# The output product of a convolution branch as seven block products, with its weights' parts kept in DRAM

## The reference, cut to what matters

```
h = rmsnorm(x);  proj = h @ W_in + b_in            # conv_val | conv_gate | pool_in | gate_a | gate_b
u  = causal_dwconv_31(conv_val * sigmoid(conv_gate))
ya = silu(layernorm(u)) @ conv_w_out               # branch A: the product that is changed
yb = (pooling branch) * scale
merged = sigmoid(gate_a) * ya + sigmoid(gate_b) * yb
x = x + merged @ mix_w_out;  x = x + gdfn(rmsnorm(x));  out = rmsnorm(x)
```

## Time and profile before

| | us |
|---|---|
| median of three runs | 1289.86 |
| their range | 1289.23 to 1290.2 |
| the profiled execution | 1289.33 |
| its span in the trace | 1287.3 |

### The profile page before, as it was taken

How to read it: one execution, slowest core, us unless ns; L and a number is a source line. 1 busy time by engine, 2 the same in 40 slices (tenths; PEclk the granted TensorE clock), 3 DMA queues, 4 the chain that set the end, 5 groups by cost and what they waited for, 6 DMA issues and landing times.

```text
span 1287.3 us, 15571 instructions
## 1 busy us (share of the span) xinstructions
PE 1270.3 (99%) x5766; PEld 1053.8 (82%) x5766; DVE 1022.8 (79%) x1163; ACT 479.5 (37%) x691; POOL 871.1 (68%) x579
## 2 busy tenths in 40 slices
PE   8999999999999999999999999999999999999997
PEld 8888888888888778877888888888888888888887
DVE  5898989999999784589677767677666779887975
ACT  6211221213234580143445343343344445424551
POOL 4536637665787833478739977877887876567861
PEclk9999999999999999999999999999999999999999
DMA  9411121214334372344212322332232259868923
GB/s 352 149 33 49 34 82 49 82 33 164 99 99 149 130 290 69 114 155 164 102 39 90 123 107 92 121 121 88 93 117 107 90 175 361 332 243 290 367 87 131
DMA packets 66408, 179.26 MB, mean 139 GB/s; under 512 B 4896, under 2 KB 13088, under 8 KB 62496
## 3 DMA queue, kind: packets, MB, share of 16 engines
q1 hardware_dynamic: 61888, 167.82, 36.2%
q10 hardware_dynamic: 4448, 10.49, 2.2%
HBM read 137.14 MB, written 41.16 MB: 139 GB/s over the span
## 4 chain that ended last, share of the span: by engine, by line
PE 90%; DVE 4%; ACT 2%; issue 2%; POOL 1%; DMA 1%; SPq 0%; DVEq 0%; POOLq 0%; ACTq 0%
PE ps L2494 30%; PE ps L2495 30%; PE ps L2496 30%; DMA cv<-in_x 1%; DVE h_lo L2092 1%; POOL w_lo L1037 1%; PE ps L2558 1%; ACT cv L1244 0%; PE ps L2548 0%; DVE cv L2083 0%; ACT cv_r L1626 0%; DVE hi_f L2004 0%; POOL w_lo L1170 0%; DVE res L2271 0%; DVE res L2187 0%
## 5 line engine op out<-in xcount | busy, mean ns | idle before, releaser
L2494 PE MATMUL ps<-h_lo,w_hi 128*128 128x512 f32 (+1 forms) x900 | 348.0, 387 | 4.5 <-DVE h_lo L1838 1.9
L2496 PE MATMUL ps<-h_hi,w_hi 128*128 128x512 f32 (+1 forms) x900 | 345.9, 384 | 0.0
L2495 PE MATMUL ps<-h_hi,w_lo 128*128 128x512 f32 (+1 forms) x900 | 345.9, 384 | 0.0
L2494 PEld LDWEIGHTS ps<-h_lo,w_hi 128*128 128x128 f32 x900 | 169.0, 188 | 41.8 <-DVE h_lo L1838 3.1
L2496 PEld LDWEIGHTS ps<-h_hi,w_hi 128*128 128x128 f32 x900 | 169.0, 188 | 33.9
L2495 PEld LDWEIGHTS ps<-h_hi,w_lo 128*128 128x128 f32 x900 | 169.1, 188 | 33.1
L1918 DVE SCALAR_TENSOR_TENSOR ps<-tmp,par,ps 128x512 f32<-128x512 f32 x224 | 158.5, 750 | 0.0
L965 POOL TENSOR_SCALAR w_hi<-raw 128x1024 fp32r<-128x1024 f32 x32 | 36.5, 1141 | 156.1 <-issue 127.5
L2494 PE MATMUL ps<-ga_r,w_hi 128*128 128x512 f32 (+1 forms) x303 | 117.4, 388 | 0.3 <-POOL w_lo L1170 0.3
L2496 PE MATMUL ps<-cv_r,w_hi 128*128 128x512 f32 (+1 forms) x303 | 117.1, 386 | 0.0
L2495 PE MATMUL ps<-cv_r,w_lo 128*128 128x512 f32 (+1 forms) x303 | 117.0, 386 | 0.0
(11 more groups left out here) (308 smaller groups left out, 2721.3 us busy)
## 6 DMA issues: line engine op xcount, KB each, us to landing
raw<-in_wstream SPq DMA_DIRECT2D x54, 512.0 KB, 3.5
tmp<-in_wffn SPq DMA_DIRECT2D x14, 1024.0 KB, 4.7
g_kept<-res SPq DMA_DIRECT2D x21, 512.0 KB, 2.8
res<-in_wffn SPq DMA_DIRECT2D x10, 1024.0 KB, 4.8
ga_r<-g_kept SPq DMA_DIRECT2D x18, 512.0 KB, 7.0
h_lo<-g_kept SPq DMA_DIRECT2D x17, 512.0 KB, 7.5
res<-in_xT SPq DMA_DIRECT2D x7, 1024.0 KB, 5.8
g_kept<-raw SPq DMA_DIRECT2D x12, 512.0 KB, 2.9
```

The costliest lines, as they stand in the source:

```text
L2494: nc.tensor.matmul(out, a_hi, b_lo, start=start, stop=False, skip_group_check=onto)
L2495: nc.tensor.matmul(out, a_lo, b_hi, start=False, stop=False, skip_group_check=onto)
L2496: return nc.tensor.matmul(out, a_hi, b_hi, start=False, stop=stop, skip_group_check=onto)
```

## The change

Branch A's output product becomes seven block products too, for four pairs of output tiles: 28 of 12 matmuls. What it needs:

- **Weights.** The sums S and the parts of all 28 are made during the first stages: eight half blocks (`PREP_SLOTS`), each loaded by SP, four sums and seven low parts on GpSimd (`prep_sum_of`, `prep_low`) on 128 by 256 values, stored by SP into `prep_kept_t`. The places between the splits are fixed by `PREP_SLOTS` and `PREP_ENDS`. During the product SP loads each block product's high and low parts (2 x 256 KB) into a ring of four.
- **High parts of the chunks** of the first stages go from GpSimd to ScalarE (`split_high`), and so do part of the prep's (`prep_highs`).
- **Order on TensorE.** P1 for the four pairs, P2 for the four, then P6, P5, P7, P4, P3 for pairs 0 and 1, and the same for 2 and 3. In SP's order `gates_back(0)` waits until all twelve low parts of z are made.
- **Data.** The T operands of z are made by VectorE, their high parts by ScalarE. VectorE forms the four result quarters from the banks (`conv_u2_of`, `conv_c22`, `conv_c21`, `conv_c12`) and merges half tiles; the gates (`a_kept_t`) come back from DRAM in 256 KB pieces.
- The mixer's block products get other places, and their sums for the first two blocks are made earlier.

```diff
+PREP_SLOTS, PREP_ENDS = (5, 7, 9, 11, 14, 18, 21, 24), (6, 7, 10, 11, 15, 19, 23, 25)
+PREP_BY_ACT = (1, 2, 4, 6, 7)
+PREP_SEQ = (P1, P2, P4, P5, P7, P6, P3)
+PREP_FIRST, PREP_LAST = PREP_SEQ[:3], PREP_SEQ[3:]
...
+            def keep_prep(x, *ps):
+                i, h = x // 2, x % 2
+                for p in ps:
+                    k = prep_n(x, p)
+                    sp.wait_ge(prep_lo, k + 1)
+                    sp.dma_start(prep_dram[CONV_SEQ.index((p, i)), :, :, h * (HALF // 2):(h + 1) * (HALF // 2)],
+                                 prep_place(k).bitcast(f32).rearrange("p (t n) -> p t n", t=2)).then_inc(prep_kept[k % PREP_PLACES], 16)
...
-            load_chunks(2, FIRST_GATE // 2 - 1)
+            load_prep(0)
+            load_early(N_FIRST, FIRST_GATE - 2)
             sp.wait_ge(w_split, FIRST_GATE - 3)
             load_weights(FIRST_GATE - 2)
+            keep_slot(FIRST_GATE - 4)
             sp.wait_ge(gb_done, PAIR0)
             sp.wait_ge(y_kept, 16 * 2)
             sp.dma_start(y_dram[:, 0:2, :], tiles(res, 0, 2)).then_inc(y_kept, 16)
...
+            def load_conv(*ops):
+                for p, i in ops:
+                    n = conv_op(p, i)
+                    r = n - GATE_OPS
+                    sp.wait_ge(f_used, n - MIX_SLOTS + 1)
+                    for t, w_t in enumerate((w_hi, w_lo)):
+                        sp.dma_start(conv_ring(w_t, n).bitcast(f32), prep_dram[r, :, t, :]).then_inc(cv_w[r % MIX_SLOTS], 16)
...
+            load_conv((P6, 0), (P6, 1))
+            for j in range(4):
+                gates_back(j)
+            load_conv((P5, 0), (P5, 1), (P7, 0))
...
+            def prep_first(x):
+                pool.wait_ge(prep_raw, 16 * (x + 1))
+                prep_sum_of("S1", x)
+                prep_low(x, P1)
+                prep_sum_of("S3", x)
+                prep_low(x, P2)
+                prep_sum_of("S2", x)
+                prep_low(x, P4)
+                prep_sum_of("S4", x)
...
-            pairs(N_OUT, (((f_post, gate_posted(GP - 2, "c12")),),
-                          ((s1_out, gates_read(GP - 1, 1)), (f_post, gate_posted(GP - 1, "c21")))), co_m, h_hi, h_lo,
-                  lambda h, k: (z_lo, KT * h + k + 1))
+            for i in range(MP):
+                pe.wait_ge(*((f_post, gate_posted(GP - 2, "c21")), (f_post, gate_posted(GP - 2, "c12")),
+                             (s1_out, gates_read(GP - 2, 1)), (s1_out, gates_read(GP - 1, 1)))[i])
+                conv_product(P1, i, ready=(lambda k: (z_lo, k + 1)) if i == 0 else None)
+            for i in range(MP):
+                pe.wait_ge(f_v1, GP + i + 1)
+                conv_product(P2, i, False, ready=(lambda k: (z_lo, 4 + k + 1)) if i == 0 else None)
```

More of the change, by code:

```diff
@@ new lines, with prep_n, prep_stores, conv_posted @@
+PREP_TOPS = NP7 * len(PREP_SLOTS) - PREP_HIGHS
+def prep_n(x, p):
+    return NP7 * x + PREP_SEQ.index(p)
+def prep_stores(place, n=NP7 * len(PREP_SLOTS)):
+    return sum(k % PREP_PLACES == place for k in range(n))
+CONV_POSTS = [(what, a + i) for a in (0, 2) for group in (("u2",), ("u3", "c22"), ("c21",), ("c12",))
+              for i in range(2) for what in group]
+def conv_posted(what, i):
+    return len(POSTS) * GP + CONV_POSTS.index((what, i)) + 1
+MERGES = [(what, a + i) for a in (0, 2) for what in ("c11", "c22", "c21", "c12") for i in range(2)]
@@ L424, in gate_out @@
         def gate_out(c, h):
-            if c == KT - 1:
-                return tile(ga, c, *span(h))
-            return odd_out[:, :] if h and c % 2 else second_half(hi_f, h)
+            return odd_out[:, :] if h and c % 2 and c < KT - 1 else second_half(hi_f, h)
         def pooled(c):
@@ new lines, in _ @@
+            conv_u2_of(0)
+            conv_t_low("T3")
+            conv_u2_of(1)
+            conv_t_low("T4")
+            merge("c11", 0)
+            merge("c11", 1)
+            for i in range(2):
+                conv_c22(i)
+                merge("c22", i)
+            for i in range(2):
+                conv_c21(i)
+                merge("c21", i)
+            for i in range(2):
+                conv_c12(i)
+                merge("c12", i)
+            conv_u2_of(2)
+            merged_low(0, 0)
@@ new lines, in _ @@
+            merged_low(1, 0)
+            conv_u2_of(3)
+            merge("c11", 2)
+            merge("c11", 3)
+            merged_low(2, 0)
+            merged_low(3, 0)
+            merged_low(4, 0)
+            merged_low(6, 0)
+            for k in range(4):
+                mix_t_sum_of("T1", k)
+            conv_c22(2)
+            merge("c22", 2)
+            conv_c22(3)
+            merge("c22", 3)
+            conv_c21(2)
+            merge("c21", 2)
+            conv_c21(3)
+            merge("c21", 3)
@@ L2739, in _, with conv_product @@
-            pairs(N_OUT, (((f_post, gate_posted(GP - 2, "c12")),),
-                          ((s1_out, gates_read(GP - 1, 1)), (f_post, gate_posted(GP - 1, "c21")))), co_m, h_hi, h_lo,
-                  lambda h, k: (z_lo, KT * h + k + 1))
+            def conv_product(p, i, first=True, ready=None):
+                n = conv_op(p, i)
+                r = n - GATE_OPS
+                pe.wait_ge(cv_w[r % MIX_SLOTS], 32 * (r // MIX_SLOTS + 1))
+                hi, lo = conv_ring(w_hi, n), conv_ring(w_lo, n)
+                for k in range(4):
+                    if ready:
+                        pe.wait_ge(*ready(k))
+                    mm = three(conv_bank(p, i), hi[:, k * P:(k + 1) * P], lo[:, k * P:(k + 1) * P],
+                               *conv_moving(PRODUCTS[p].partition("*")[2], k), first and k == 0, k == 3, not first)
+                mm.then_inc(f_used, 1)
```

799 lines of the change are left out of this document (551 added, 248 removed), and 4 rows, old and new, of the table MIX_ADDS.

## The result

The changed kernel takes 1307.81 us in the median (1304.77 to 1308.96, 4 runs), the kernel before 1289.78 (1289.23 to 1290.2, 4 runs). The ratio is 1.0138, 95% interval 1.0126 to 1.015: it is slower by 18 us, where 7 us less was forecast, and outside the range. One execution of all those reported here, of the kernel of experiment 7, took 2132.56 us at a mean granted clock of 0.556, and no comparison uses it.

A forecast was written before the change was run, and what follows sets the result against it. TensorE, 99% busy, was taken to bound the kernel. From 1289.3 us the terms -10.9, -1.0, -0.8, +5.0, +0.7 and +0.5 gave 1282.8, left at 1283; 8-in-10 range 1277 to 1289, the forecast's own 1280 to 1286.

The forecast's parts named there:

- the sum's silent start: Whole kernel: the sum starts from the profiled 1289.3 us and takes off 48 matmuls at 0.227 us each.
- sign of being wrong as a whole: TensorE's waits from 30 to 650 us summing to more than 10 us or to less than 3.
- Term 1: Branch A's output product: 336 matmuls instead of 384, at 0.227 us each, -10.9 us.
- Term 2: Start of branch A's output product: the 1.04 us wait on a low part of z goes, -1.0 us.
- Term 3: Entry to the mixer's products: the 0.87 us wait for low parts of weights shrinks through earlier sums, -0.8 us.
- Term 4: T loads on SP: prep stores delay them, VectorE runs late, TensorE stalls at `gate_u2(0)` and the mean matmul, +5.0 us.
- Term 5: Supply of the new product: P5's weights land late behind SP's wait at `gates_back(0)`, +0.7 us, bounds 0 and 4.
- Term 6: First stages: GpSimd's added prep work fits its idle time, splits almost all in time, +0.5 us, bounds 0 and 3.
- The slower rival: New product: DMA starves the block products, deciding from about 270 GB/s down; 18 us more at 250, end 1300; chance 0.10.
- The first rival: T loads: they are no loss, term 4 is 0 to 2 us, time 1276 to 1280; chance 0.22.
- a fit of the Trainium skill: T loads: 2.0 us plus bytes over 436 GB/s, store 4.4 us, both loads 6.8, term 4 about 1.5, end 1279.3.

The follow-up runs named there:

- experiment 7: Kernel of experiment 6 plus one 256 KB copy within DRAM for each block product of the new product: 1286.82 us, ratio 0.9981 to the kernel before.
- aligned kernel: Changed kernel with its SBUF tensors allocated in another order, so every product operand starts at a multiple of 128 bytes: 1288.08 us, ratio 0.9993 to the kernel before.
- experiment 5: Aligned kernel with SP's loads of the T operands ahead of the three prep stores: 1283.05 us, ratio 0.9949 to the kernel before.
- experiment 6: Kernel of experiment 5 with P5's weights for pairs 0 and 1 issued ahead of the first four gate loads: 1281.77 us, ratio 0.993 to the kernel before.
- experiment 10: Kernel of experiment 6 with half block 3's three first high parts on ScalarE and pooled tile 6 reloaded later: 1295.25 us, ratio 1.0045 to the kernel before.
- experiment 11: Kernel of experiment 6 with half block 3's last four parts made behind chunk 13's split, not chunk 11's: 1285.11 us, ratio 0.9968 to the kernel before.
- the first kernel: First of two kernels of matmuls alone, 22 groups of 24 at different byte offsets: 0.228 us per matmul with both operands at 32, 0.233 with weights elsewhere.

## Why the prediction was wrong

For each stage, what TensorE's starts lie apart beyond 0.227 us, added up over its timeline (only steps over 0.26 us: waits, the restarts behind them, and the slow clock), in us:

| stage (us) | before | changed | aligned | + T loads early | + P5 early |
|---|---|---|---|---|---|
| first stages, 30 to 345 | 0.1 | 0.8 | 2.5 | 2.6 | 2.8 |
| 345 to 370 | 0 | 1.9 | 5.05 | 0 | 0 |
| rest of the gates, to 467 | 3.7 | 3.5 | 3.6 | 3.6 | 3.6 |
| new product, to 545 | 1.7 | 3.4 | 3.0 | 3.5 | 2.3 |
| mixer, to 640 | 2.45 | 2.5 | 1.75 | 1.8 | 1.7 |
| later, to 1250 | 1.7 | 0.2 | 1.8 | 1.5 | 1.5 |

- **The step that failed** is the sum's silent start: "1289.3" less 48 matmuls takes for granted that the other 5718 keep their 0.227 us. They don't. Changed and aligned kernel differ by 21.3 us of span; the aligned one loses 5.4 us more to waits (17.7 against 12.3 in the table), so the longer distance costs 26.7 us, 4.7 ns for each matmul. The starts say the same: between 30 and 1250 us the mean of all steps under 0.26 us is 0.2320 us in the changed kernel and 0.2269 in the aligned one. The prediction named the cost of each edit of work and left out one that moves no work: 8 columns more on two tensors. Its own sign of being wrong as a whole, waits over 10 us or under 3 between 30 and 650 us, could not catch this: they are 8.4 us.
- **Term 1** holds with the addresses right: 48 matmuls less, 0.227 us each.
- **Term 2** (-1.0): the wait is gone; the new product's first matmuls start without one.
- **Term 3** (-0.8): 2.45 to 1.75, -0.7.
- **Term 4** (+5.0): +5.05 in the aligned kernel, at the named place and from the named cause, as experiment 5 shows. That the size fits so well is in part luck. The loads went out at 301.98 us, as forecast; but the store had taken 4.6 us (6.4 forecast), and VectorE could start only 11.4 us behind the loads' issue (8.1 forecast). VectorE's first T sum began 9.0 us later than before the change and `gate_u2(0)` ended 6.7 us later (5 forecast), so 2.3 us were given back (2.5 forecast). TensorE itself came 2.7 us later than before, so with the 0.7 us of slack its wait is 3.4 us, and 1.65 of slow clock behind it, which the prediction didn't have, fill up the sum. At the mean matmul nothing more was lost.
- **Term 5** (+0.7): mis-sized. The stage lost 3.0 us where before, with its one wait, lost 1.7: +1.3, and with term 2's 1.0 taken out +2.3; the P5 wait that was named is 0.8 to 1.3 us of it, and the rest are waits of 0.1 to 0.3 on weights, with the slower steps behind them.
- **Term 6** (+0.5): mis-sized, +2.4, and from three causes. "The others have over 1 us" counted GpSimd's operations but not when the half blocks land: half block 3 landed 4.4 us after its issue in the kernel of experiment 6, 2.6 of them idle on GpSimd, and the splits behind it cost 0.7 us at 155 and 166 us. At 251 us 0.8 us go to a small product whose read-out stands on ScalarE behind the high parts that the change put there. And at 336 us 0.9 us go to a low part of a split that took 4.4 us where 2.4 were counted.
- **Together**, with the measured terms: 1289.3 - 10.9 - 1.0 - 0.7 + 5.05 + 2.3 + 2.4 = 1286.5; the profiled execution of the aligned kernel has 1287.38. So had the addresses been kept, the median, 1288.08 us, would have been in the range for 8 in 10 (1277 to 1289), but 5 us above the forecast, outside the forecast's own 1280 to 1286, and no gain that can be told from none.
- **The rivals.** The slower rival gave chance 0.10 to an outcome that came, but by the wrong mechanism: DMA averages 305 GB/s over the stage in the changed kernel (475 to 550 us) and 326 in that of experiment 6, above the 270 that it needed to decide, though single stretches lie under it (263 GB/s from 467 to 475 us in experiment 6). VectorE held TensorE up in the new product once, 0.8 us at 549.7 us of the changed kernel. The first rival, no loss at the T loads, is out by experiment 5. The prediction set beside it a fit of the Trainium skill (DMA: Bandwidth & Descriptors, Anatomy of one DMA) that the page gives for DMAs issued by GpSimd; here SP issues them. The 4.4 us that it gives for the store are near the 4.6 measured, the 6.8 for the two loads are not near 11.4.

## What to carry to other kernels

When a diff changes the size of any SBUF tensor, compare the start addresses of each product's moving operand and weights before and after, keep their difference at a multiple of 256 bytes, and read the distance of matmul starts before looking for waits: the busy share hardly tells (99% before, 98% after). A wait put into one engine's queue stops all that stands behind it, so a copy or a store moved there is priced by what it waits for, and late operands cost twice when TensorE's pause brings the slow clock.

## What the runs showed of the hardware

Two things were not expected. **The distance between fast float32 matmuls of 512 columns depends on how the moving operand and the weights lie to each other in a partition:** 0.227 us (0.229 with a group's first matmuls) where the starts differ by a multiple of 256 bytes, or 16 bytes less, and 0.231 to 0.237 in nearly all other groups, up to 4%, with nothing else running. The exceptions leave the full rule open: 0.229 at a difference of 64 (modulo 256) in three groups, with 0.233 in two others, and 0.229 at one of 124 in the first kernel. The Trainium skill (TensorE: Matmul & The Clock Gate, Step-by-step: what each phase is for) gives the moving operand and the weight load a read port each, so that a load takes nothing from a running matmul. These runs show that where the two lie against each other matters all the same; whether it is their reads that meet, they don't show. **DMA and GpSimd traffic did not lengthen it:** 112 matmuls in 25 us at 43 and at 158 GB/s.

The lower clock doesn't go by the length of TensorE's pause alone in these rows. Steps of 3.61 us between two starts (aligned kernel, 359.3 us), 2.50 (experiment 10, 550.3 us) and 2.35 (experiment 7, 518.7 us) were followed, at once or within 1 us, by seven or eight steps slower than 0.35 us, most of them 0.427, at granted clocks of 0.72, 0.76 and 0.83 over windows of 6, 7 and 10 us. Steps of 2.65 (changed kernel, 511.4 us) and 2.54 us (experiment 11, 178.7 us) were followed by none.
